# Normalization by thirds among the last down-projections of a two-layer decoder trunk

## The reference, cut to what matters

```
def layer_norm(x, g, b):
    mu = mean(x); var = mean((x - mu)**2)
    return (x - mu) * rsqrt(var + 1e-5) * g + b

for i in (0, 1):
    shift, scale, gate = mods[i, 0]            # adaLN, from the conditioning vector
    h = x * (1 + scale) + shift
    m = s5_mixer(h) if i == 0 else short_conv_mixer(h)
    x = layer_norm(ALPHA * x + gate * m)
    shift, scale, gate = mods[i, 1]
    h = x * (1 + scale) + shift
    f = (gelu(conv3(h @ w_up)[gate half]) * conv3(h @ w_up)[value half]) @ w_down   # causal, 3 taps
    x = layer_norm(ALPHA * x + gate * f)

short_conv_mixer(h): z = h @ w_in; return (z_b * conv3(z_c * z_v)) @ w_out
```

## Time and profile before

| what | us |
|---|---|
| median of 3 runs | 2614.55 (2613.03 to 2614.8) |
| profiled execution, its own time | 2612.22 |
| its span, first to last instruction | 2610.4 |
| PE busy | 2440.3 |
| DVE busy | 1442.7 |
| POOL busy | 1125.0 |
| ACT busy | 630.1 |
| mean granted TensorE clock | 0.970 |

### The profile page before, as it was taken

How to read it: one execution, slowest core, us unless ns; L and a number is a source line. 1 busy time by engine, 2 the same in 40 slices (tenths; PEclk the granted TensorE clock), 3 DMA queues, 4 the chain that set the end, 5 groups by cost and what they waited for, 6 DMA issues and landing times.

```text
span 2610.4 us, 37019 instructions
## 1 busy us (share of the span) xinstructions
PE 2440.3 (93%) x15428; PEld 2328.4 (89%) x15428; DVE 1442.7 (55%) x1959; ACT 630.1 (24%) x1271; POOL 1125.0 (43%) x615
## 2 busy tenths in 40 slices
PE   6796999699999999999979999897999999999995
PEld 5786999499999999999859999886999999999994
DVE  8787222755555555566583254367455655555555
ACT  5232211331222222222131101104322222222213
POOL 6976333263343444434245333325544444444420
PEclk9898999799999999999989999998999999999998
DMA  7445433021121222222002221100111111111102
GB/s 266 144 138 170 150 105 113 0 73 59 63 81 66 81 81 81 73 81 73 33 20 58 81 73 49 41 33 17 49 49 42 49 49 49 41 49 49 46 20 72
DMA packets 90813, 187.28 MB, mean 72 GB/s; under 512 B 27680, under 2 KB 49952, under 8 KB 90400
## 3 DMA queue, kind: packets, MB, share of 16 engines
q1 hardware_dynamic: 81120, 175.23, 20.6%
q10 hardware_dynamic: 9536, 9.77, 1.1%
HBM read 170.66 MB, written 14.32 MB: 71 GB/s over the span
## 4 chain that ended last, share of the span: by engine, by line
PE 84%; DVE 9%; DVEq 2%; POOL 2%; POOLq 2%; ACT 1%; issue 1%; DMA 0%; SPq 0%; ACTq 0%
PE bank L661 18%; PE bank L663 17%; PE bank L662 17%; PE bank L920 8%; PE bank L921 7%; PE bank L922 7%; PE bank L939 2%; PE bank L625 1%; DVE X L1750 1%; DVE ROWS L1742 1%; DVE HL L1778 1%; DVE X L1736 1%; PE bank L640 1%; PE bank L641 1%; PE bank L631 1%
## 5 line engine op out<-in xcount | busy, mean ns | idle before, releaser
L661 PE MATMUL bank<-HH,WH 128*128 128x344 f32 x2880 | 924.6, 321 | 0.0
L662 PE MATMUL bank<-HL,WH 128*128 128x344 f32 x2880 | 920.1, 319 | 0.0
L663 PE MATMUL bank<-HH,WL 128*128 128x344 f32 x2880 | 920.0, 319 | 0.0
L488 POOL TENSOR_TENSOR WH<-RAW,ZERO 128x1024 fp32r<-128x1024 f32 x176 | 372.0, 2114 | 1195.0 <-DMA RAW<-in_wstream 1079.1
L1716 DVE SCALAR_TENSOR_TENSOR X<-bank,MOD,X 128x344 f32<-128x344 f32 (+1 forms) x624 | 355.5, 571 | 428.2 <-PE bank L922 293.4
L661 PEld LDWEIGHTS bank<-HH,WH 128*128 128x128 f32 x2880 | 541.0, 188 | 15.1 <-issue 13.4
L663 PEld LDWEIGHTS bank<-HH,WL 128*128 128x128 f32 x2880 | 541.4, 188 | 0.0
L662 PEld LDWEIGHTS bank<-HL,WH 128*128 128x128 f32 x2880 | 541.0, 188 | 0.0
L483 POOL TENSOR_TENSOR WL<-RAW,WH 128x1024 fp32r<-128x1024 f32 x188 | 499.9, 2659 | 31.4 <-ACT WH L1032 17.5
L920 PE MATMUL bank<-GH,WH 128*128 128x344 f32 x1248 | 410.1, 329 | 22.3 <-DVE X L1716 22.3
L921 PE MATMUL bank<-GL,WH 128*128 128x344 f32 x1248 | 403.1, 323 | 0.0
(11 more groups left out here) (286 smaller groups left out, 2409.2 us busy)
## 6 DMA issues: line engine op xcount, KB each, us to landing
RAW<-in_wstream SPq DMA_DIRECT2D x188, 512.0 KB, 3.6
ADA<-in_wada SPq DMA_DIRECT2D x20, 2048.0 KB, 9.2
FST<-in_wada SPq DMA_DIRECT2D x8, 1024.0 KB, 8.7
out_yT<-X SPq DMA_DIRECT2D x3, 1376.0 KB, 5.6
FST<-in_xT SPq DMA_DIRECT2D x8, 512.0 KB, 5.1
UT<-s_u SPq DMA_DIRECT2D x8, 512.0 KB, 4.2
s_y<-YG ACTq DMA_DIRECT2D x8, 512.0 KB, 3.1
FST<-s_y SPq DMA_DIRECT2D x8, 512.0 KB, 8.5
```

The lines of the kernel that those rows point to most:

```text
L488: ptt(WH[:, slot, :], RAW[:, slot, :], bc(ZERO[:, :], [128, 1024]), add).then_inc(s_hi, 1)
L661: pe.matmul(o, wh, hh, start=k == 0, stop=False)
L662: pe.matmul(o, wh, hl, start=False, stop=False)
L663: m = pe.matmul(o, wl, hh, start=False, stop=k == KC - 1)
```

## The change

The last two pairs A and B of each phase are laid among one another third by third (A1 A0 B0 A2 B1 B2), with five banks in a ring in place of two (banks 0, 1, 2, 6, 7), and means 0 and 1 and variance 0 stand between them. Mean 2 follows; variances 1 and 2 stand among the first matmuls of the next phase. That phase starts with four units in place of two, all four on third 0, then on 1, then on 2. `users()` therefore frees the slots of these four only in third 2, and that of pair A as soon as A2 is done. Centring, squares, scaling and modulation go by halves of four feature chunks. ScalarE writes h twice, rounded (HH) and in full (FST); the vector engine and GpSimd subtract one half each (`low_h`). ScalarE splits the high part of the next phase's first four units (`high_half`), GpSimd only their low part. The vector engine makes the constants earlier, behind the last convolution of the phase. GpSimd scales X by ALPHA in eight operations of 1032 columns, after it has split units 4 and 5 of the new phase. The root's table is loaded ahead. The constant stores and loads for the second ConvFFN move on ScalarE from behind normalization 1 to behind hidden chunk 1.

```diff
 # users(): which matmuls free each unit's slot
-                seq = [(s_up, 3 * (up + i + 1)) for i in range(ups)]
-                seq[0] = seq[1]
+                seq = [(s_up, 3 * up + 9 + i if i < 4 else 3 * (up + i + 1)) for i in range(ups)]
...
-                    seq += [(s_down, dn + 24 * g)] * 2
+                    seq += [(s_down, dn + 24 * g + (8 if g == groups - 1 else 0))] * 2
 # GpSimd
-            def residual(li):
-                for t in range(3):
...
-                    for k in range(KC):
-                        xk = X[:, k, TH * t:TH * (t + 1)]
-                        m = pool.tensor_scalar(xk, xk, LC[:, 2, k:k + 1], LC[:, 3, k:k + 1], ALU.mult, ALU.add)
+            def low_h(li, t):
+                w = TH if t < 2 else PT2
+                c = slice(TH * t, TH * t + w)
+                pool.wait_ge(s_hh, 2 * (3 * li + t) + 1)
+                ptt(HL[:, 0:4, c], FST[:, 1, 0:4, c], HH[:, 0:4, c].bitcast(F32), sub).then_inc(s_hlo, 1)
+            def alpha_x(li):
+                pool.wait_ge(s_h, 3 * li + 3)
+                for k in range(KC):
+                    m = pool.tensor_scalar(X[:, k, :], X[:, k, :], LC[:, 2, k:k + 1], LC[:, 3, k:k + 1], ALU.mult, ALU.add)
+                m.then_inc(s_xup, 1)
+            def norm(li, n0):
+                if li < 3:
+                    low_half(n0)
+                    low_half(n0 + 1)
+                    low_h(li, 0)
+                    low_half(n0 + 2)
+                    low_half(n0 + 3)
+                    low_h(li, 1)
+                    low_h(li, 2)
+                    straight(n0 + 4, n0 + 6)
+                    alpha_x(li)
 # TensorE
+            def end_of_phase(li, nA, cA, gA, gB):
...
+                last_downs(li, 0, sA, gA, 1, range(KC))
+                last_downs(li, 8, sA, gA, 0, range(KC))
...
+                last_downs(li, 16, sB, gB, 0, range(KC))
+                last_downs(li, 24, sA, gA, 2, range(3))
+                pe.wait_ge(s_ev, 3 * up)
+                mean(li, 0)
+                last_downs(li, 24, sA, gA, 2, range(3, KC))
+                last_downs(li, 32, sB, gB, 1, range(6))
+                variance(li, 0)
+                last_downs(li, 32, sB, gB, 1, range(6, KC))
+                last_downs(li, 40, sB, gB, 2, range(3))
+                mean(li, 1)
+                last_downs(li, 40, sB, gB, 2, range(3, KC))
+                last_mean(li)
+            def first_four(li, n0, u0):
+                for t in range(3):
+                    for q in range(4):
+                        slot = (n0 + q) % 4
+                        if t == 0:
+                            pe.wait_ge(s_unit, n0 + q + 1)
...
+                        elif q < 2:
+                            pe.wait_ge(s_ev, 3 * u0 + 2 * (t - 1) + q + 1)
+                        if q == 0:
+                            pe.wait_ge(s_h, 3 * li + t + 1)
+                            pe.wait_ge(s_hlo, 3 * li + t + 1)
+                        o = (BK[6 + q] if q < 2 else BK[3 * (q - 2) + t])[:, 0:TH]
+                        for k in range(KC):
+                            if k == 4 and t == 0:
+                                if li and q == 1:
+                                    variance(li, 1)
+                                if q == (3 if li else 1):
+                                    variance(li, 2)
+                            m = chunk(o, slot, k, t)
+                        m.then_inc(s_up, 1)
 # ScalarE
+            def norm(li, n0, first_rows):
+                act.activation(STAB[:, :], EPST[:, :], ACT.Sqrt)
+                squares(li, 0)
+                if li:
+                    deviation(li, 0)
+                    high_half(n0)
+                    high_half(n0 + 1)
...
+                modulate(li, 0)
+                if li:
+                    squares(li, 1)
+                    high_half(n0 + 2)
+                    high_half(n0 + 3)
+                    deviation(li, 1)
+                    first_rows(0)
+                    squares(li, 2)
+                    modulate(li, 1, (0,))
+                    deviation(li, 2)
+                    modulate(li, 1, (1,))
...
+                modulate(li, 2)
+                first_rows(1)
+                first_rows(2)
 # VectorE
+            def norm(li, gsec):
+                take_last(li, gsec, 16, 0, range(KC))
+                take_last(li, gsec, 24, 2, range(3))
+                center(li, 0, 0)
+                take_last(li, gsec, 24, 2, range(3, 5))
+                center(li, 0, 1)
+                take_last(li, gsec, 24, 2, range(5, KC))
+                take_last(li, gsec, 32, 1, range(5))
+                deviation(li, 0)
+                scale(li, 0, 0)
+                take_last(li, gsec, 32, 1, range(5, 7))
+                scale(li, 0, 1)
+                take_last(li, gsec, 32, 1, range(7, KC))
+                take_last(li, gsec, 40, 2, range(4))
+                center(li, 1, 0)
+                take_last(li, gsec, 40, 2, range(4, 6))
+                center(li, 1, 1)
+                take_last(li, gsec, 40, 2, range(6, KC))
+                end_down(gsec)
...
-                    dve.wait_ge(s_ev, 3 * (u0 + 1 + vg) + 6 * cc)
+                    dve.wait_ge(s_ev, 3 * (u0 + 2) if first else 3 * (u0 + 1 + vg) + 6 * cc)
```

More of the change, by code:

```diff
@@ L29 @@
 KC = 8
-KD = 5
 SEQ = 1024
@@ L1026, in _ @@
+            variance(3, 2)
         @block.scalar
@@ new lines, in squares, with deviation @@
+            def squares(li, t):
+                if li and t == 1:
+                    act.wait_ge(s_down, LAST[li] + 48)
+                for h in range(2):
+                    act.wait_ge(s_cent, 2 * (3 * li + t) + h + 1)
+                    act.activation(LSQ[t][:, 4 * h:4 * h + 4], X[:, 4 * h:4 * h + 4, TH * t:TH * (t + 1)], ACT.Square).then_inc(s_sq, 1)
+            def deviation(li, t):
+                act.wait_ge(s_var, 3 * li + t + 1)
+                act.activation(LTMP[t][1], BK[3 + t][:, 0:TH], ACT.Sqrt, bias=EPST[:, :]).then_inc(s_sd, 1)
@@ new lines, in ffn_row @@
+            def ffn_row(c, vg, t, b, batch):
+                Tr, Ur = (T0, U0) if vg == 0 else (T1, U1)
+                row = 2 * c + vg
+                cwr = CWF[:, :, :, :].rearrange("p a b c -> p (a b) c")
+                act.activation(Ur[:, 2 + TH * t:2 + TH * (t + 1)], b[:, 0:TH], ACT.Copy)
+                if t == 2:
+                    act.activation(FB[:, row, :], b[:, TH - 10:TH], ACT.Copy)
+                    if vg == 0 and batch is not None:
+                        take_mods(batch, b)
+                act.activation(Tr[:, TH * t:TH * (t + 1)], b[:, 0:TH], ACT.Identity,
+                               bias=cwr[:, row, 3:4], scale=cwr[:, row, 2:3]).then_inc(s_ev, 1)
@@ L1293, in ffn_rows, with ffn_first_rows @@
+            def ffn_first_rows(u0, late, t):
+                if t == 0:
+                    act.wait_ge(s_late, late)
+                for vg in range(2):
+                    act.wait_ge(s_up, 3 * u0 + 4 * t + vg + 1)
+                    ffn_row(0, vg, t, BK[6 + vg], None)
             def ffn_rows(c, u, rows_done, batch):
@@ L1795, in layer_norm @@
-                if not last:
-                    split(0)
-                scale(2)
-                if not last:
-                    split(1)
-                    split(2)
+                    dve.tensor_copy(HH[:, :, SEQ:NT], SMP[:, 0])
+                    fence()
+                    tt(HL[:, :, SEQ:NT], SMP[:, 0], HH[:, :, SEQ:NT].bitcast(F32), S_)
+                dve.wait_ge(s_hh, 2 * (3 * li + t) + 2)
+                tt(HL[:, 4:KC, c], FST[:, 1, 4:KC, c], HH[:, 4:KC, c].bitcast(F32), S_).then_inc(s_h, 1)
@@ new lines, in first_norm @@
+            def first_norm():
+                for t in range(2):
+                    for h in range(2):
+                        center(0, t, h)
+                deviation(0, 0)
+                for h in range(2):
+                    scale(0, 0, h)
+                for h in range(2):
+                    center(0, 2, h)
+                deviation(0, 1)
+                for h in range(2):
+                    scale(0, 1, h)
+                low_h(0, 0)
+                deviation(0, 2)
+                for h in range(2):
+                    scale(0, 2, h)
+                low_h(0, 1)
+                low_h(0, 2)
```

434 lines of the change are left out of this document (212 added, 222 removed).

## The result

The changed kernel takes 2632.07 us (median of 4 runs, 2631.01 to 2635.55) against 2614.68 (4 runs, 2613.03 to 2617.41): ratio 1.0068, 95% interval 1.0050 to 1.0085. It is slower by 17.4 us. The forecast was 2650 in 2612 to 2664: sign right, rise half as large as foreseen. Its profiled execution took 2632.64 us.

A forecast was written before the change was run, and what follows sets the result against it. TensorE was taken as the bound, losing time where phases hand over. Hand-over and end gains -21.8, ConvFFN unit 4 costs +26.3 and +24.5, short convolution +7.9 sum to +36.9: 2650 us, range 2612 to 2664.

The forecast's parts named there:

- the sign, its place and its cause: Slower by 36.9 us, mainly unit 4 of both ConvFFNs, waiting on chunk 0's chain as vector operations take turns with GpSimd.
- each ends just as a GpSimd operation ends: Convolution of chunk 0: two-input vector operations from SBUF and GpSimd's operations take turns, one whole operation each.
- Gate row, each of its four after 1.8: Chunk 0's gate convolution in a ConvFFN: each of four operations follows a 1.8 us GpSimd scaling, ending 13.1 after E.
- the second wait at unit 6: In a ConvFFN, chunk 1 meets the same turns against unit splits: TensorE waits about 2 us (0 to 4).
- the 5.9 at unit 5 of the short convolution: TensorE waits 5.9 us at unit 5, whose chain meets GpSimd some 7 times.
- The 7.9 of that phase: Short convolution's total cost: the wait of 5.9 us at unit 5 plus clock 2 (bounds 0 and 8).
- 2.5 for a wait over 4 us: Lower TensorE clock after a wait costs 2.5 us if it exceeds 4 us, 1.5 after a shorter one.
- The hand-overs: Gains between phases of 6.0, 4.9 and 6.7 us, and 4.2 at the end, each to plus or minus 4.
- rival B: Half-way: scaling X takes far less than 1.8 a row, ConvFFN wait 12, short convolution 2: 2625 us; chance 0.22.
- A's condition: Rival A, turns hardly cost: decided if ConvFFN waits stay under some 6 us each; 2606 to 2611 us; chance 0.15.
- D's late units 6 and 7: Rival D, knock-on: scaling X makes units 6 and 7 late, 5 us in each of three phases: 2666; chance 0.08.
- the prediction's 5.8 us: TensorE's wait for unit 4 in a ConvFFN without any collision, as unit 1 ends only 7.5 us before unit 3.

The follow-up runs named there:

- the takes first: Against the changed kernel, the vector engine takes all eight chunks of pair B third 1 before waiting for deviation 0: 2617.67 us, ratio 1.0017.
- the new order of their steps: Units 0 and 1 finish the last third before 2 and 3; with four other edits on the changed kernel 2581.88 us, without this order 2589.68.

## Why the prediction was right, and where it was half off

**Right: the sign, its place and its cause.** Unit 4 of both ConvFFNs starts late, released by ScalarE's row of chunk 1, and the chain in front of it is stretched by GpSimd. VectorE, GpSimd and one row of ScalarE in the changed kernel, first ConvFFN:

```profile
550.15 1.69 DVE L1961 SCALAR_TENSOR_TENSOR ROWS<-ROWS,CWF 128x1024 f32<-128x1024 f32 x1 [16.15 <-ACT ROWS L1371]
551.77 2.35 DVE L1962 SCALAR_TENSOR_TENSOR ROWS<-STF,CWF,ROWS 128x8 f32<-128x8 f32 x1
554.19 1.78 DVE L1964 SCALAR_TENSOR_TENSOR ROWS<-STF,CWF,ROWS 128x8 f32<-128x8 f32 x1
555.89 1.27 DVE L1965 SCALAR_TENSOR_TENSOR ROWS<-ROWS,CWF 128x1024 f32<-128x1024 f32 x1
557.09 3.36 DVE L1961 SCALAR_TENSOR_TENSOR ROWS<-ROWS,CWF 128x1024 f32<-128x1024 f32 x1
560.37 0.22 DVE L1962 SCALAR_TENSOR_TENSOR ROWS<-STF,CWF,ROWS 128x8 f32<-128x8 f32 x1
560.67 0.86 DVE L1964 SCALAR_TENSOR_TENSOR ROWS<-STF,CWF,ROWS 128x8 f32<-128x8 f32 x1
561.46 1.29 DVE L1965 SCALAR_TENSOR_TENSOR ROWS<-ROWS,CWF 128x1024 f32<-128x1024 f32 x1
563.88 2.12 DVE L1970 TENSOR_TENSOR ROWS<-ROWS 128x1032 f32<-128x1032 f32 x1 [1.13 <-ACT ROWS L1394]
567.13 1.23 DVE L1950 TENSOR_TENSOR GL<-ROWS,GH 128x1032 fp32r<-128x1032 f32 x1 [1.13 <-ACT GH L1396]
```

```profile
548.87 1.89 POOL L491 TENSOR_TENSOR WH<-RAW,ZERO 128x1024 fp32r<-128x1024 f32 x1 [17.76 <-DMA RAW<-in_wstream]
550.84 3.25 POOL L486 TENSOR_TENSOR WL<-RAW,WH 128x1024 fp32r<-128x1024 f32 x1
554.05 1.89 POOL L491 TENSOR_TENSOR WH<-RAW,ZERO 128x1024 fp32r<-128x1024 f32 x1
556.02 3.34 POOL L486 TENSOR_TENSOR WL<-RAW,WH 128x1024 fp32r<-128x1024 f32 x1
559.35 14.54 POOL L608 TENSOR_SCALAR X<-X,LC 128x1032 f32<-128x1032 f32 x8
...
568.75 0.63 ACT L1371 ACTIVATE ROWS<-bank,CWF 128x344 f32<-128x344 f32 x1
```

VectorE's value convolution was to begin at E - 6.4 (E the end of unit 3's last matmul, 556.5) and it does, at 550.15. Then come the turns of the earlier trace rows: L1962 ends at 554.12, just as the split of 550.84 does (554.09), L1964 at 555.97 with the next (555.94). An operation of 1024 columns ends some 1.1 us after the split, since its own work is still to come (560.45 and 559.36); the prediction's "each ends just as a GpSimd operation ends" holds for those of 8 columns only. This is the whole-instruction lock of the Trainium skill, page SBUF — State Buffer, section SBUF: two separate sides; the trace agrees. One row does not follow from it: L1962 at 560.37 takes 0.22, though a scaling of GpSimd is under way from 559.35 to 561.52.

**Mis-sized: "Gate row, each of its four after 1.8".** This is the largest part of what makes 20 of 12.9. Expected were 3.5 (end of the value convolution), 13.1 (gate), 16.1 (product), 19.1 (low half), 20.1 (first row) behind E. Measured: 0.7, 6.3, 9.5, 11.9, 12.9. Of the 7.2 us too many, 4.0 are the gate row's, whose four took 5.66 us instead of 9.6, and 2.8 the value row's. Two things were wrong in the gate row. First, the length of a scaling: three times the 0.61 of a 344-column one gave 1.8, and the trace has

```profile
L608 POOL TENSOR_SCALAR X<-X,LC x24: 1194/2167/2295, 559.4 to 1862.0; 128x1032 f32<-128x1032 f32 x24
```

(ns, shortest, median, longest): 1.2 when free, 2.2 beside a vector operation, which is 1.2 and a wait. Second, that every one of the four waits a turn: of four back to back, L1962 takes 0.22 and L1965 1.29; only the first (3.36, behind the last split) and L1964 (0.86) lose anything. In the value row, too, one turn fewer came than was counted: L1965 goes at 555.89, 0.1 us ahead of the next split. The run with X unscaled shows how little hangs on the scaling here: 0.6 us of the gate row, and 0.3 of the wait, since the next splits come sooner and take back at the low half what the product gains. With two of the four splits gone the scaling moves up instead, and nothing is gained either. So what holds the chain is GpSimd's full queue, whichever operation comes next in it; that splits hold it longer than scalings is read from the traces.

**Absent: the second wait at unit 6** (2 us, 0 to 4), and the 5.9 at unit 5 of the short convolution was 0.78, which I put down to the same overcount of the turns. The 7.9 of that phase came out as 8.8 by another way, the stores: a right sum with a wrong reason, which is luck. The step that failed here is that the stores and loads, named among what the change moves, were given no price; they cost 7.8 us.

**Clock.** 2.5 for a wait over 4 us: 17.3 less 14.8 is 2.5, 15.0 less 13.05 is 1.95, 7.8 less 4.77 is 3.0. Right to half a microsecond.

**The hand-overs.** 6.7, 6.4 and 6.7 for 6.0, 4.9 and 6.7; the waits of the second one were 4.26, 5.38, 3.17 and 4.94 for 4.4, 5.9, 3.5 and 4.9. One was off: mean 1, which was to wait 2.6, waited 0.38, and the gain was 1.5 us larger. At the end 1.4 came of 4.2. Variance 2, which the prediction had freed there, still waited 3.11 for its squares (7.90 before), and chunk 37 and mean 1 waited 3.14 and 1.26 in the queue behind the deviation; the takes first give back 2.7 there.

**The rivals.** 2632 lies between the forecast, whose own range began at 2637, and B's 2625, and nearer to B: B's wait of 12 is about what came (12.9 to the first row), and its 2 us for the short convolution would have been right (1.0) without the stores. With the wait for the stores moved a chunk later the kernel takes 2624.97 us, B's 2625. So rival B, at 0.22, fits the ConvFFNs better than the forecast at 0.50, and what brings 2632 nearer to the forecast is 7.8 us behind the stores, which neither had counted. A's condition, under some 6 us at each ConvFFN, fails in the changed kernel; D's late units 6 and 7 are absent, the ledger is flat behind unit 4.

**Open.** How much the constants alone are worth in time, and how short chunk 0's chain would be with no split beside it: a version without the splits of units 4 and 5 was not run, so that they cost what they seem to is read from the traces only. The run with two units also releases the first slots sooner, so it shows what four units cost, but not how much of it is the shorter distance (the prediction's 5.8 us) and how much the splits that fall into the chain.

## What to carry to other kernels

Work that hides a chain hides it by its distance: before an order is changed, write down for each chain what runs beside it, for the old and for the new order, and check the queue behind each moved wait, DMA waits too. A change that loses can hold the larger gain: here four units third by third, with the new order of their steps, were worth 17 us once four waits that the change had uncovered were moved out of the way, each by a line or two of order. And a ledger of the n-th instruction's start between two traces finds such a wait even where a total over lines hides it.

## What the runs showed of the hardware

- GpSimd's in-place tensor_scalar takes 0.61 us for 344 columns but only 1.20 for 1032, not three times as much; by estimate some 0.3 us are fixed. The run with X unscaled has a third point: 0.34 for 8 columns.
- Of two vector operations back to back, the second, of 8 columns, is not always held by GpSimd: L1962 at 560.37 takes 0.22 while a scaling is under way (begun at 559.35, 2.17 long), but 2.35 at 551.77 while a split is (begun at 550.84, 3.25 long). What decides which is not shown.
- A store of 176 KB took 13.5 us to land when a 2 MB load had been issued 0.45 us before it, and 6.1 when that load came 3.5 us after it. In the run with the wait a chunk later it took 13.4, with the load 1.7 us before it.
